# Attention over pairs of units: ScalarE instead of VectorE multiplies the second unit's probabilities by one over their sum

## The chip, the core and the metric

The kernel runs on one core of a Trainium2 chip, in one launch. The core has a matrix engine (TensorE, PE in the profile; its weight loads are PEld), three engines for elementwise work (VectorE or DVE, ScalarE or ACT, GpSimd or POOL) and a queue engine that issues transfers (SyncE, SP). Each runs its own list of instructions in order, and they wait for one another through semaphores. The metric is the device time of one execution in microseconds. Everything is computed in float32.

## The reference, cut to what matters

Two transformer layers over 256 latent tokens and 256 context tokens. Each layer has an attention, a recurrent half beside it, an output projection, and a mixture of experts, whose weights are most of the 497 MB that are read. What the change touches is the softmax of both attentions:

```python
def full_attention(q, k, v):                     # layer 0
    sc = jnp.einsum('bqhd,bkhd->bhqk', q, k).astype(F32) * q.shape[-1] ** -0.5
    p = jax.nn.softmax(sc, axis=-1).astype(v.dtype)
    return jnp.einsum('bhqk,bkhd->bqhd', p, v)

def window_attention(q, k, v, k_ctx, v_ctx, sink):   # layer 1
    ...
        p = jax.nn.softmax(jnp.concatenate([sk, s_ctx, s_band], axis=-1), axis=-1).astype(v.dtype)
        return (jnp.einsum('bkgqc,bckd->bqkgd', p[..., 1:1 + n_ctx], v_ctx)
                + jnp.einsum('bkgqs,bskd->bqkgd', p[..., 1 + n_ctx:], vi))
```

In layer 1 the window is applied by adding a mask to the scores, and a sink logit adds one more term to the sum of the exponentials.

## The kernel before, in words

The program is a chain of stages. Each is one block with a barrier at its end, so a stage starts when the last engine has finished the one before, and the loads of expert weights that a stage issues start with it. The two attention stages are calls of one function, `attention_stage` (L861).

A unit is one head and one tile of 128 queries. Layer 0 has 32 units: for the first 16 all 512 keys count ("wide"), for the other 16, whose queries are context tokens, only 256 ("narrow"). Layer 1 has 16 units of 512 keys. Two neighbouring units form a pair, the even unit first. A unit goes through these steps:

- `score` (L911): PE multiplies queries by keys into one of four PSUM banks (the trace shows four matmuls for a pair).
- `maximum` (L984): VectorE takes the row maximum (L995) and turns it into the bias of the exponential (L997; L1002 and L1003 where there is a sink). In layer 1 it first adds the mask (L991).
- `exponential` (L960): ScalarE takes the exponential and sums each row (L965); with a sink, one more small exponential (L968).
- normalisation (L1022 and L1023): VectorE takes the reciprocal of the sum (`den`) and multiplies the 128 rows of probabilities by it.
- `turn` (L918): PE transposes the probabilities, 128 by 128 at a time (L923). It waits for the multiplied probabilities.
- copy (L977): ScalarE copies the transposed probabilities out of PSUM.
- `values` (L926): PE multiplies them by the values of the pair (L933), and `copy_out` on VectorE takes the result out (L1009).

The order on each engine is written out by hand. PE, per round j: the scores of the next pair (2j+2, 2j+3), the turns of this pair (2j, 2j+1), the values of the pair before (j-1). In layer 0, in six of the rounds, PE also does a product for later modulation rows (L194), and VectorE adds its bias (L202, L206). ScalarE alternates: copy of unit u, exponential of unit u+2. VectorE, for each unit u: reciprocal and multiplication of u, then maximum of u+2; after the odd unit also the `copy_out` of the pair before.

Of the kernel before, what the change touches and what calls it, by code (L numbers as in the profile page):

```python
# [20 lines left out]
ALU = mybir.AluOpType  # L21
ACT = mybir.ActivationFunctionType
AX = mybir.AxisListType

P = 128
# [5 lines left out]
T = NT * P  # L31
# [21 lines left out]
class Chain:  # L53
# [6 lines left out]
    def step(self, ins):  # L60
        self.n += 1
        ins.then_inc(self.sem, 1)
        self.engine.wait_ge(self.sem, self.n)
# [797 lines left out]
def attention_stage(c, units, qt, kt, v_of, scale, dst_t, p, pt, width, sink=None, mask=None, sp_work=None, md=None):  # L861
# [4 lines left out]
    nc = c.nc  # L866
    n = len(units)
    pairs = n // 2
    scored, masked, nmax_r, exp_r, p_ready, turned, pt_ready, product, out_r = (
        c.sem(x) for x in ("scored", "masked", "negative_max", "exp_done", "probs_ready", "probs_turned", "probs_t_copied", "pv_product", "attn_copied"))  # L870
    den_r = c.sem("sink_exp")
    ada_after = {}
    if md:
        ada_after = {3 + a * (pairs - 6) // (md.n - 1): a for a in range(md.n)}
# [3 lines left out]
    nm, rs, es = ([c.stat[:, a + s:a + s + 1] for s in range(4)] for a in (0, 4, 8))  # L878

    def keys(u):  # L880
        return range(units[u][2], NT)

    with nc.Block() as block:
        @block.sync
        def _(sp):
            if md:
                for a in range(len(md.ring)):
                    if a == 1:
                        sp.wait_ge(tables_in, 16 * md.n_loads)
                    md.load_weights(sp, a, ada_in[a])  # L890
            if sp_work:
                sp_work(sp)
            if md:
                R = len(md.ring)
                for a in range(R, md.n):
                    sp.wait_ge(ada_product, a - R + 1)
                    md.load_weights(sp, a, ada_in[a % R])
                sp.wait_ge(ada_done, md.n)
                md.store(sp, stored)
                sp.wait_ge(stored, 16 * md.Q * len(md.segments))  # L900
# [8 lines left out]
        @block.tensor  # L909
        def _(pe):  # L910
            def score(u):  # L911
                h, t, k0 = units[u]
                if u >= 4:
                    pe.wait_ge(exp_r, u - 3)
                nc.tensor.matmul(c.ps[u % 4][:, k0 * P:T], qt[0:width, h, t * P:(t + 1) * P], kt(h)[0:width, k0 * P:T],
                                 start=True, stop=True).then_inc(scored, 1)

            def turn(u):  # L918
                pe.wait_ge(p_ready, u + 1)
                if u >= 2:  # L920
                    pe.wait_ge(pt_ready, u - 1)
                for k in keys(u):
                    last = nc.tensor.transpose(c.bank(4 + u % 2, 4, P)[:, k, :], p[:, u % 4, k * P:(k + 1) * P], c.ident[:])  # L923
                last.then_inc(turned, 1)

            def values(j):  # L926
                pe.wait_ge(pt_ready, 2 * j + 2)
                if j:
                    pe.wait_ge(out_r, j)
                for k in keys(2 * j):  # L930
                    for half in range(2):
                        u = 2 * j + half
                        last = nc.tensor.matmul(c.ps[6][half * 64:half * 64 + 64, 0:P], v_of(units[u][0], k), pt[:, u % 4, k, :],  # L933
                                                start=k == units[u][2], stop=k == NT - 1)
                last.then_inc(product, 1)

            score(0)
            score(1)
            for j in range(pairs):
                for u in (2 * j + 2, 2 * j + 3):  # L940
                    if u < n:
                        score(u)
                turn(2 * j)
                turn(2 * j + 1)
                if j:
                    values(j - 1)
                if j in ada_after:
                    a = ada_after[j]
                    if a == 0:
                        pe.wait_ge(columns, 1)  # L950
                    else:
                        pe.wait_ge(ada_done, a)
                    pe.wait_ge(ada_in[a % len(md.ring)], 16 * (a // len(md.ring) + 1))
                    md.product(a, 7).then_inc(ada_product, 1)
            values(pairs - 1)

        @block.scalar
        def _(act):
            def exponential(u):
                h, t, k0 = units[u]  # L960
                s = u % 4
                act.wait_ge(nmax_r, u + 1)
                if u >= 4:
                    act.wait_ge(turned, u - 3)
                nc.scalar.activation(p[:, s, k0 * P:T], c.ps[s][:, k0 * P:T], ACT.Exp, bias=nm[s], scale=scale,  # L965
                                     accum_out=rs[s]).then_inc(exp_r, 1)
                if sink is not None:
                    nc.scalar.activation(es[s], nm[s], ACT.Exp, bias=sink[:, h:h + 1]).then_inc(den_r, 1)  # L968

            exponential(0)  # L970
            exponential(1)
            for u in range(n):
                act.wait_ge(turned, u + 1)
                if u >= 4:
                    act.wait_ge(product, u // 2 - 1)
                k0 = units[u][2]
                nc.scalar.activation(pt[:, u % 4, k0:NT, :], c.bank(4 + u % 2, 4, P)[:, k0:NT, :], ACT.Copy).then_inc(pt_ready, 1)  # L977
                if u + 2 < n:
                    exponential(u + 2)

        @block.vector
        def _(dve):
            step = c.dve_chain.step
# [22 lines left out]
            def copy_out(j):  # L1006
                h, t, _ = units[2 * j]
                dve.wait_ge(product, j + 1)
                nc.vector.tensor_copy(dst_t[:, h // 2, t * P:(t + 1) * P], c.ps[6][:, 0:P]).then_inc(out_r, 1)  # L1009
# [5 lines left out]
            for u in range(n):  # L1015
                k0 = units[u][2]
                dve.wait_ge(exp_r, u + 1)
                den = rs[u % 4]
                if sink is not None:
                    dve.wait_ge(den_r, u + 1)  # L1020
                    step(nc.vector.tensor_tensor(den, den, es[u % 4], ALU.add))
                step(nc.vector.reciprocal(den, den))  # L1022
                nc.vector.tensor_scalar(p[:, u % 4, k0 * P:T], p[:, u % 4, k0 * P:T], den, None, ALU.mult).then_inc(p_ready, 1)  # L1023
                if u + 2 < n:
                    maximum(u + 2)
                j = u // 2
                if u % 2 and j:
                    copy_out(j - 1)
                    if j - 1 in ada_after:
                        if ada_after[j - 1] == 0:  # L1030
                            dve.wait_ge(tables_in, 16 * md.n_loads)
                        dve.wait_ge(ada_product, ada_after[j - 1] + 1)
                        md.finish(ada_after[j - 1], 7, ada_done)
# [1278 lines left out]
```

## Time and profile before

| what | value |
|---|---|
| median of three runs | 1686.78 us (1683.6 to 1687.5) |
| the profiled execution: its time, its span | 1687.27 us, 1685.5 us |
| mean granted TensorE clock over the span | 0.865 of full speed |
| PE, PEld busy | 1249.5 us (74%), 727.4 us (43%) |
| DVE, ACT, POOL busy | 541.3 us (32%), 405.3 us (24%), 39.3 us (2%) |
| layer 0's attention stage | from about 256 to 335 us |
| layer 1's attention stage | from about 1099 to 1161 us |

The two stages are 141 us of the span, 8%. In most of the rest the DMA share is 0.9 or more: the experts' weights are streamed. Inside the attention stages no weights of experts are loaded (the loads of layer 0's stage are modulation weights and the output projection), so shares over the whole span say little about them; they are read with views cut to their stretch. In a timeline row the idle time in brackets is what the engine waited just before the row, and what ended the wait.

### The profile page before, as it was taken

To read this page: it belongs to the slowest core of one execution; us is meant where nothing else is said; L and a number is where in the kernel's file an instruction comes from. 1 tells how busy PE (TensorE), PEld (TensorE's weight loads), DVE (VectorE), ACT (ScalarE), POOL (GpSimd) and SP (SyncE) were. 2 spreads that over 40 slices of the span, in tenths; PEclk is the share of its full clock that TensorE was granted. 3 is DMA by queue.
4 is the path that set the end of the run, shared out by engine and by line. 5 is a ranking of instruction groups with operands and counts; after the bars stand their busy time and mean duration, and the time that the engine had idled before them with its cause. 6 is when DMAs were issued, how large, how long until landed. Compare 5 with 4: busy or idle time off the path is not lost. (4 is left out here: it accounts for less than half of the span.)

```text
span 1685.5 us, 34940 instructions
## 1 busy us (share of the span) xinstructions
PE 1249.5 (74%) x14230; PEld 727.4 (43%) x14231; DVE 541.3 (32%) x1492; ACT 405.3 (24%) x932; POOL 39.3 (2%) x83
## 2 busy tenths in 40 slices
PE   3897888795799997686762999488497675556552
PEld 2454665543465554343431565244255342223221
DVE  0537555515322221121115444863521110111102
ACT  0343224303132321121104123342222221111110
POOL 0001001010000000000002000000000000000000
PEclk8899899997899998899875999758699897777776
DMA  6411988396699999999987210442689999999995
GB/s 254 156 76 45 329 331 305 106 408 254 254 415 428 429 430 428 429 429 429 429 354 256 68 50 0 168 182 88 257 365 428 429 429 429 429 429 429 429 429 217
DMA packets 84160, 515.12 MB, mean 306 GB/s; under 512 B 13917, under 2 KB 18242, under 8 KB 58746
## 3 DMA queue, kind: packets, MB, share of 16 engines
q1 hardware_dynamic: 75248, 489.63, 70.9%
q10 hardware_dynamic: 5146, 13.78, 2.1%
q0 software_dynamic: 3696, 10.73, 1.7%
q8 instruction: 50, 0.82, 0.2%
q14 instruction: 20, 0.16, 0.0%
HBM read 497.10 MB, written 17.01 MB: 305 GB/s over the span
## 5 line engine op out<-in xcount | busy, mean ns | idle before, releaser
L1481 PE MATMUL bank<-sb_ring,sb_scratch 128*32 128x256 f32 x3904 | 271.8, 440 | 150.7 <-DMA sb_ring<-in_moe_w_up 139.3
L1481 PEld LDWEIGHTS bank<-sb_ring,sb_scratch 128*32 128x32 f32 x3904 | 146.4, 126 | 273.6 <-issue 214.2
L1562 DVE TENSOR_TENSOR sb_scratch<-sb_scratch,bank 128x128 f32<-128x128 f32 x88 | 25.4, 288 | 701.2 <-ACT sb_scratch L1515 701.2
L1519 ACT ACTIVATE sb_scratch<-bank 32x256 f32<-32x256 f32 x352 | 131.8, 374 | 273.9 <-PE bank L1491 270.8
L1481 PE MATMUL bank<-sb_scratch 128*32 128x256 f32 x1728 | 117.5, 432 | 63.4 <-DMA sb_scratch<-in_moe_w_up 58.4
L1461 PE MATMUL bank<-sb_h,sb_scratch 128*32 128x256 f32 x2256 | 141.2, 385 | 6.1 <-DVE sb_scratch L1549 6.1
L1515 ACT ACTIVATE sb_scratch<-bank 128x128 f32<-128x128 f32 x88 | 24.4, 277 | 424.5 <-PE bank L1481 424.4
L1491 PE MATMUL bank<-sb_ring,sb_scratch 128*32 128x256 f32 x1856 | 111.5, 380 | 8.6 <-issue 8.2
L1481 PEld LDWEIGHTS bank<-sb_scratch 128*32 128x32 f32 x1728 | 61.5, 124 | 117.9 <-issue 92.7
L1461 PEld LDWEIGHTS bank<-sb_h,sb_scratch 128*32 128x32 f32 x2256 | 75.0, 111 | 54.6 <-DVE sb_scratch L1549 6.6
L1491 PEld LDWEIGHTS bank<-sb_ring,sb_scratch 128*32 128x32 f32 x1856 | 62.7, 110 | 51.2 <-issue 19.0
L1882 PE MATMUL bank<-sb_ht,sb_ring 128*128 128x512 f32 (+1 forms) x192 | 69.2, 521 | 0.0
L556 PE MATMUL bank<-sb_ht,sb_ring 128*128 128x512 f32 x128 | 55.3, 593 | 1.4 <-PEq L311 1.4
L1491 PE MATMUL bank<-sb_scratch 128*32 128x256 f32 x864 | 51.9, 380 | 4.6 <-issue 4.1
L1554 DVE STREAM_TRANSPOSE sb_scratch<-bank 128x256 f32<-128x256 f32 x90 | 38.9, 432 | 37.4 <-PE bank L1461 37.4
L1882 PEld LDWEIGHTS bank<-sb_ht,sb_ring 128*128 128x128 f32 x192 | 36.3, 190 | 31.3 <-issue 29.6
L194 PE MATMUL bank<-sb_ring 128*32 128x128 f32 x1280 | 40.2, 282 | 6.7 <-DMA sb_ring<-in_ada_w 6.7
L1066 PE MATMUL bank<-sb_ring,sb_scratch 128*128 128x512 f32 x96 | 43.2, 592 | 0.0
L194 PEld LDWEIGHTS bank<-sb_ring 128*32 128x32 f32 x1280 | 35.4, 113 | 13.5 <-DMA sb_ring<-in_ada_w 7.7
L1515 ACT ACT_TABLE_LOAD x21 | 26.9, 1283 | 56.3 <-issue 38.8
L1491 PEld LDWEIGHTS bank<-sb_scratch 128*32 128x32 f32 x864 | 29.2, 110 | 24.6 <-issue 9.7
L556 PEld LDWEIGHTS bank<-sb_ht,sb_ring 128*128 128x128 f32 x128 | 24.2, 190 | 31.6 <-issue 31.6
(366 smaller groups left out, 1450.4 us busy)
## 6 DMA issues: line engine op xcount, KB each, us to landing
sb_ring<-in_moe_w_gate SPq DMA_DIRECT2D x44, 2048.0 KB, 27.4
sb_ring<-in_moe_w_up SPq DMA_DIRECT2D x44, 2048.0 KB, 32.1
sb_ring<-in_moe_w_down SPq DMA_DIRECT2D x41, 2048.0 KB, 34.5
sb_ring<-in_ada_w SPq DMA_DIRECT2D x20, 2048.0 KB, 14.4
sb_scratch<-in_moe_w_up SPq DMA_DIRECT2D x20, 2048.0 KB, 35.7
sb_scratch<-in_moe_w_gate SPq DMA_DIRECT2D x20, 2048.0 KB, 29.9
sb_scratch<-in_moe_w_down SPq DMA_DIRECT2D x20, 2048.0 KB, 36.2
sorted_out<-sb_scratch ACTq DMA_DIRECT2D x88, 128.0 KB, 6.1
```

The lines of the kernel that those rows point to most:

```text
L194: last = self.c.nc.tensor.matmul(self.c.ps[bank][32 * q:32 * q + 32, 0:P], self.condk[:, k, :], w[:, k, q * P:(q + 1) * P], start=k == 0, ...
L556: last = nc.tensor.matmul(c.ps[u % NB][:, 0:rhs.shape[1]], lhs, rhs, start=k == 0, stop=k == KC - 1)
L1066: last = nc.tensor.matmul(c.ps[u % 4][:], src, wo[:, k, q * BANK:(q + 1) * BANK], start=k == 0, stop=k == KC - 1)
L1461: last = nc.tensor.matmul(c.ps[0][MB * q:MB * q + MB, 0:DQ], m.pick[:, t, :], c.h[:, t, q * DQ:(q + 1) * DQ], start=t == 0, stop=t == nt - 1)
L1481: last = nc.tensor.matmul(c.bank(1, 2, FQ)[MB * q:MB * q + MB, :, :], m.xt[:, k, :], m.gu[j][:, :, k, q * FQ:(q + 1) * FQ], start=k == 0, ...
L1491: last = nc.tensor.matmul(c.ps[3][MB * q:MB * q + MB, 0:DQ], m.hmt[:, k, :], down[k][:, q * DQ:(q + 1) * DQ], start=k == 0, stop=k == DE / ...
L1515: nc.scalar.activation(m.sg, c.ps[1][:, 0:FQ], ACT.Silu).then_inc(silu_r, 1)
L1519: last = nc.scalar.activation(m.yb[j][:, q * DQ:(q + 1) * DQ], c.ps[3][MB * q:MB * q + MB, 0:DQ], ACT.Copy)
L1554: v.transpose(m.xt, c.bank(0, MB, KC).rearrange("p j k -> p k j")).then_inc(xt_ready, 1)
L1562: v.tensor_tensor(m.hm, m.sg, c.ps[1][:, FQ:2 * FQ], ALU.mult).then_inc(hm_ready, 1)
L1882: last = nc.tensor.matmul(c.ps[bank_of(u)][:, 0:rhs.shape[1]], lhs, rhs, start=k == 0, stop=k == KC - 1)
```

## The change

For every odd unit VectorE only takes the reciprocal (after.py L1036) and signals it through a new semaphore, `inverse_sum`. ScalarE waits for it, multiplies the probabilities in place by the reciprocal (`divide`, after.py L977 to L980: a Copy whose scale is the column of reciprocals) and signals `odd_probs_ready`, for which PE's turn of an odd unit now waits. The even units stay as they were. ScalarE's list is written in another order, by pairs. The line numbers after L966 move by 2 to 16.

```diff
             def turn(u):
-                pe.wait_ge(p_ready, u + 1)
+                pe.wait_ge(odd_ready if u % 2 else p_ready, u // 2 + 1)
...
-            exponential(0)
-            exponential(1)
-            for u in range(n):
+            def copy_turned(u):
                 act.wait_ge(turned, u + 1)
                 if u >= 4:
                     act.wait_ge(product, u // 2 - 1)
...
-                if u + 2 < n:
-                    exponential(u + 2)
+
+            def divide(u):
+                k0 = units[u][2]
+                act.wait_ge(inverse_r, u // 2 + 1)
+                nc.scalar.activation(p[:, u % 4, k0 * P:T], p[:, u % 4, k0 * P:T], ACT.Copy, scale=rs[u % 4]).then_inc(odd_ready, 1)
+
+            exponential(0)
+            exponential(1)
+            divide(1)
+            for j in range(pairs):
+                copy_turned(2 * j)
+                if j + 1 < pairs:
+                    exponential(2 * j + 2)
+                    exponential(2 * j + 3)
+                copy_turned(2 * j + 1)
+                if j + 1 < pairs:
+                    divide(2 * j + 3)
...
-                step(nc.vector.reciprocal(den, den))
-                nc.vector.tensor_scalar(p[:, u % 4, k0 * P:T], p[:, u % 4, k0 * P:T], den, None, ALU.mult).then_inc(p_ready, 1)
+                if u % 2:
+                    nc.vector.reciprocal(den, den).then_inc(inverse_r, 1)
+                else:
+                    step(nc.vector.reciprocal(den, den))
+                    nc.vector.tensor_scalar(p[:, u % 4, k0 * P:T], p[:, u % 4, k0 * P:T], den, None, ALU.mult).then_inc(p_ready, 1)
```

ScalarE's list in layer 0's attention, wide units, over two rounds, before (L965 is the exponential, L977 the copy of turned probabilities; `sb_scratch` holds the probabilities, `sb_stat` their sums):

```order
L977 ACTIVATE sb_h<-bank 128x512
L965 ACTIVATE sb_scratch,sb_stat<-bank,sb_stat 128x512
L977 ACTIVATE sb_h<-bank 128x512
L965 ACTIVATE sb_scratch,sb_stat<-bank,sb_stat 128x512
L977 ACTIVATE sb_h<-bank 128x512
L965 ACTIVATE sb_scratch,sb_stat<-bank,sb_stat 128x512
```

and after, in the same place (L975 is the copy, L980 the new multiplication):

```order
L980 ACTIVATE sb_scratch<-sb_scratch,sb_stat 128x512
L975 ACTIVATE sb_h<-bank 128x512
L965 ACTIVATE sb_scratch,sb_stat<-bank,sb_stat 128x512 x2
L975 ACTIVATE sb_h<-bank 128x512
L980 ACTIVATE sb_scratch<-sb_scratch,sb_stat 128x512
```

One instruction per pair is added, it stands ahead of the even unit's copy, and the two exponentials now stand together between the two copies.

VectorE's list in the same stretch, before (L1022 the reciprocal, L1023 the multiplication, L995 and L997 the maximum, L1009 the copy out):

```order
L1009 COPY sb_h<-bank 128x128
L1022 RECIPROCAL sb_stat<-sb_stat 128x1
L1023 TENSOR_SCALAR sb_scratch<-sb_scratch,sb_stat 128x512
L995 TENSOR_REDUCE sb_stat<-bank 128x1
L997 TENSOR_SCALAR sb_stat<-sb_stat 128x1
L1022 RECIPROCAL sb_stat<-sb_stat 128x1
L1023 TENSOR_SCALAR sb_scratch<-sb_scratch,sb_stat 128x512
L995 TENSOR_REDUCE sb_stat<-bank 128x1
L997 TENSOR_SCALAR sb_stat<-sb_stat 128x1
```

and after (L1036 is the odd unit's reciprocal, L1038 and L1039 the even unit's reciprocal and multiplication, L1008 and L1010 the maximum, L1022 the copy out):

```order
L1022 COPY sb_h<-bank 128x128
L1038 RECIPROCAL sb_stat<-sb_stat 128x1
L1039 TENSOR_SCALAR sb_scratch<-sb_scratch,sb_stat 128x512
L1008 TENSOR_REDUCE sb_stat<-bank 128x1
L1010 TENSOR_SCALAR sb_stat<-sb_stat 128x1
L1036 RECIPROCAL sb_stat<-sb_stat 128x1
L1008 TENSOR_REDUCE sb_stat<-bank 128x1
L1010 TENSOR_SCALAR sb_stat<-sb_stat 128x1
```

The odd unit's multiplication is gone; its reciprocal still stands behind the maximum of the next even unit.

## Rows read from the trace of the kernel before

**Rows 1.** Windows: both attention stages, then three stretches of layer 1's.
```profile
core 0: us, PE busy (x) PEld busy (x) DVE busy (x) ACT busy (x) POOL busy (x), PEclk, DMA share, GB/s
256.00:335.00 79.00, 66.20 (x736) 43.16 (x736) 45.36 (x155) 34.56 (x97) 5.40 (x10) 0.96 0.59 215
1099.00:1161.00 62.00, 54.07 (x227) 30.27 (x228) 35.75 (x120) 24.68 (x66) 0.00 (x0) 0.64 0.24 102
1117.65:1125.33 7.68, 7.68 (x31) 4.17 (x29) 4.44 (x15) 2.79 (x8) 0.00 (x0) 0.50 0.01 2
1140.50:1143.50 3.00, 2.23 (x8) 0.79 (x6) 2.43 (x9) 0.73 (x2) 0.00 (x0) 1.00 0.00 0
1144.00:1147.00 3.00, 3.00 (x21) 2.34 (x21) 1.15 (x4) 1.67 (x6) 0.00 (x0) 0.50 0.00 0
```

**Rows 2.** Waits in layer 0's attention: total us, times, longest us.
```profile
PEld bank L923 <- DVE sb_scratch L1023: 18.7, 24, 1.3
```

**Rows 3.** Timeline, PE, a wide round: start us, us, instruction, idle before.
```profile
269.48 1.98 PE L915 MATMUL bank<-sb_scratch,sb_ht 96*128 96x512 f32 x4
271.30 0.60 PE L923 MATMUL bank<-sb_ident,sb_scratch 128*128 128x128 f32 x4
272.41 0.66 PE L923 MATMUL bank<-sb_ident,sb_scratch 128*128 128x128 f32 x4 [0.51 <-DVE sb_scratch L1023]
...
274.02 1.99 PE L915 MATMUL bank<-sb_scratch,sb_ht 96*128 96x512 f32 x4
```

**Rows 4.** Timeline, DVE, the same round.
```profile
270.65 0.69 DVE L995 TENSOR_REDUCE sb_stat<-bank 128x1 f32<-128x512 f32 x1 [0.16 <-PE bank L915]
...
271.67 0.16 DVE L1022 RECIPROCAL sb_stat<-sb_stat 128x1 f32<-128x1 f32 x1
271.87 0.49 DVE L1023 TENSOR_SCALAR sb_scratch<-sb_scratch,sb_stat 128x512 f32<-128x512 f32 x1
...
274.14 0.29 DVE L1009 COPY sb_h<-bank 128x128 f32<-128x128 f32 x1 [1.00 <-PE bank L933]
274.35 0.15 DVE L1022 RECIPROCAL sb_stat<-sb_stat 128x1 f32<-128x1 f32 x1
```

**Rows 5.** Timeline, ACT, the same round.
```profile
271.94 0.60 ACT L977 ACTIVATE sb_h<-bank 128x512 f32<-128x512 f32 x1 [2.11 <-PE bank L923]
...
273.01 0.20 ACT L965 ACTIVATION_READ_ACCUMULATOR sb_scratch<-bank,sb_stat 128x1 f32 x1
```

**Rows 6.** ACT groups by form: xcount | busy us, mean ns | idle.
```profile
L2009 ACT ACTIVATE sb_h<-sb_h 128x512 f32<-128x512 f32 x8 | 5.0, 630 | 24.0 <-DVEq L2057 24.0
...
L1645 ACT ACTIVATE sb_scratch<-sb_scratch,sb_wsel 128x1024 f32<-128x1024 f32 x4 | 4.6, 1144 | 14.4 <-DMA sb_scratch<-sorted_out,sb_slot 14.4
L1649 ACT ACTIVATE sb_h<-sb_x 128x1024 f32<-128x1024 f32 x4 | 4.2, 1052 | 1.8 <-DVE sb_x L1689 1.8
...
L1999 ACT ACTIVATE sb_scratch<-sb_scratch 128x256 f32<-128x256 f32 x7 | 3.0, 429 | 0.0
```

**Rows 7.** ACT groups by form: the copies of wide turned probabilities.
```profile
L977 ACT ACTIVATE sb_h<-bank 128x512 f32<-128x512 f32 x16 | 9.6, 597 | 19.2 <-PE bank L923 19.1
```

**Rows 8.** Timeline, DVE then ACT: a hand-over from one to the other.
```profile
208.31 0.17 DVE L428 TENSOR_SCALAR sb_stat<-sb_stat 128x8 f32<-128x8 f32 x1
...
208.51 0.21 ACT L808 ACTIVATE sb_stat<-sb_stat 128x8 f32<-128x8 f32 x1 [0.52 <-DVE sb_stat L428]
```

**Rows 9.** Timeline, DVE: the multiplication of a narrow odd unit.
```profile
312.75 0.35 DVE L1023 TENSOR_SCALAR sb_scratch<-sb_scratch,sb_stat 128x256 f32<-128x256 f32 x1
```

**Rows 10.** Timeline, PE, layer 1: a round at half clock, then a mixed one.
```profile
1117.65 3.78 PE L915 MATMUL bank<-sb_scratch 64*128 64x512 f32 x4
1121.37 2.13 PE L923 MATMUL bank<-sb_ident,sb_ring 128*128 128x128 f32 x8
...
1143.94 1.11 PE L923 MATMUL bank<-sb_ident,sb_ring 128*128 128x128 f32 x4 [1.20 <-DVE sb_ring L1023]
...
1150.80 1.12 PE L923 MATMUL bank<-sb_ident,sb_ring 128*128 128x128 f32 x4 [1.21 <-DVE sb_ring L1023]
```

**Rows 11.** Timeline, DVE, the half-clock round: the odd unit's multiplication.
```profile
1121.83 0.49 DVE L1023 TENSOR_SCALAR sb_ring<-sb_ring,sb_stat 128x512 f32<-128x512 f32 x1
```

More of the change, by code:

```diff
@@ L870, in attention_stage @@
         c.sem(x) for x in ("scored", "masked", "negative_max", "exp_done", "probs_ready", "probs_turned", "probs_t_copied", "pv_product", "attn_copied"))
-    den_r = c.sem("sink_exp")
+    den_r, inverse_r, odd_ready = c.sem("sink_exp"), c.sem("inverse_sum"), c.sem("odd_probs_ready")
     ada_after = {}
```

## The prediction

> **What bounds the kernel now.** The page says little: VectorE is busy 32% and ScalarE 24% of the span, but most of the span streams experts' weights. I cut the views to the two attention stages. By windows, layer 0's stage runs at a granted clock of 0.96 with PE busy 66 of 79 us [rows 1]. So PE is close to being the bound, and what counts is where it waits. The waits name it: weight loads of the turns (L923) wait 24 times, 18.7 us in all, for VectorE's multiplication L1023 [rows 2].
>
> The timeline of one wide round shows which multiplication. PE does the scores of the next pair, then the even unit's turn at once; then it is idle 0.51 us and starts the odd unit's turn at 272.41 [rows 3]. VectorE ended the odd unit's multiplication at 271.87 + 0.49 = 272.36 [rows 4]. That is late because VectorE, in order, first takes the maximum of the next even unit, whose scores are ready only when this round has begun: the reduce starts at 270.65 behind a wait for PE, the odd reciprocal at 271.67 [rows 4]. After the values PE goes straight into the next round, 274.02 - 269.48 = 4.54 us after this one. The loop is closed: scores, maximum, odd reciprocal, odd multiplication, odd turn, values, scores. Whatever lengthens the time from the odd reciprocal to the odd turn lengthens every round by as much. The narrow rounds and layer 1 have the same order; there PE waits 1.20 us for the odd multiplication in the later rounds [rows 10]. In layer 1's rounds at half clock PE is busy throughout [rows 1], and the two turns follow without a gap [rows 10].
>
> **The change, part by part.** Removed: 24 multiplications on VectorE (8 wide and 8 narrow in layer 0, 8 in layer 1). Added: 24 multiplications on ScalarE and a hand-over from VectorE to it. Both stand on the loop.
>
> *Old piece.* Reciprocal start to multiplication start 0.20, multiplication 0.49: 0.69 us for a wide unit [rows 4]. Narrow: the multiplication takes 0.35 [rows 9], so 0.20 + 0.35 = 0.55.
>
> *New piece.* The reciprocal itself 0.16 [rows 4]. The hand-over: VectorE ended at 208.31 + 0.17 = 208.48, ScalarE started at 208.51, so 0.03 [rows 8]. The multiplication: a wide activation from SBUF to SBUF takes 0.630; one whose scale is a column of SBUF took 1.144 against 1.052 without it at 1024 elements, so the column costs 0.09 [rows 6]. Together 0.72. Narrow: 0.429 + 0.09 = 0.52 [rows 6]. So 0.16 + 0.03 + 0.72 = 0.91 wide and 0.71 narrow: **+0.22** per wide, **+0.16** per narrow pair.
>
> *The bounds of that price.* No row has exactly this form. From below, the copy out of PSUM without a column, 0.597 [rows 7], would give 0.16 + 0.03 + 0.60 - 0.69 = +0.10 wide, and 0.429 without the column +0.07 narrow. From above, the nearest longer row of the form is the 1.144 for twice the elements [rows 6], +0.42 more for each. I take 0.72 and 0.52, because the size and the column are each shown by a pair of rows.
>
> The Trainium skill, VectorE: DVE Perf Modes, section The TRN2 errata, gives (224 + N)/1.2 ns for ScalarE from SBUF and (58 + N/2)/0.96 ns for a VectorE copy or multiplication in its double mode. For 512 that is 0.61 and 0.33, for 256 0.40 and 0.19. The trace agrees on ScalarE (0.63) and not on VectorE (0.49 and 0.35); by the page an estimate of the loss would be +0.27 and +0.20 a pair, 5.8 us where the rows give 4.6. The measured rows decide.
>
> *The sum.* Layer 0: 8 x 0.22 + 8 x 0.16 = 3.0. Layer 1: in six of its eight rounds PE waits for the odd multiplication, 6 x 0.22 = 1.3. In two half-clock rounds, as that from 1117.65, the second turn starts half way through 2.13 us, at 1122.43 [rows 10], and the multiplication had ended at 1122.32 [rows 11]: 0.11 hides half of it, 2 x 0.11 = 0.2. Sum 3.0 + 1.3 + 0.2, unrounded **+4.6 us**.
>
> *ScalarE's other work.* ScalarE was idle 2.11 us before the even copy at 271.94 [rows 5], so the multiplication finds it free. It stands ahead of that copy: reciprocal done at 271.83, ScalarE held from 271.86 for 0.72, to 272.58, so the even copy and the next even exponential come at most 0.6 us late. That exponential's sum was done at 273.21 [rows 5]; the reciprocal that needs it started at 274.35 [rows 4]. The slack of 1.14 covers 0.6. The odd copy comes behind both exponentials now; those who need it, the pair's values and the bank's next turn, stand in the next round behind its scores. Cost nothing; if that cover were gone, up to 0.6 a round.
>
> *What VectorE gains.* 0.49 us a wide unit, 0.35 a narrow one. It comes behind the odd reciprocal, so it makes the maximum of the next odd unit early, and then VectorE waits for the values anyway, 1.00 us before the copy out [rows 4]. The gain falls into that wait: nothing.
>
> *Transfers.* No transfer moves. Each stage starts its loads at its own start, behind a barrier, so the delay passes to the end whole.
>
> *The clock.* Layer 1's stage has a granted clock of 0.64 in the mean. Its early rounds run at half clock; the later ones are mixed: scores at the full 2.4 GHz (granted 1.00), and after the wait for the odd multiplication the odd turn and values at 1.2 GHz (granted 0.50) [rows 1]. A mixed round takes 1150.80 - 1143.94 = 6.86 us [rows 10], one at half clock throughout 7.68 [rows 1]. The clock fell each time around the 1.20 us wait and came back after a stretch without one. With 1.42 us of waiting and another period, I expect it to come back less often: two of the four late rounds at half clock, 2 x (7.68 - 6.86) = +1.6. Bounds: none, or all four plus the last turns and values at half rate, about +6; and below nothing, -1.6, if it comes back two rounds earlier.
>
> Forecast: 4.6 + 1.6 = **+6.2 us**. The profiled execution took 1687.27 (span 1685.5 and 1.8 around it), 0.5 above the median of 1686.78; on the median that is **1693**.
>
> **The rivals.**
> *B, only the price, no clock.* +4.6, or +2.0 with the lower price (14 x 0.10 + 8 x 0.07, and nothing in the two half-clock rounds). Then 1689 to 1691.4, within 0.3% (5.1 us, about what a measurement of this kernel tells from no change). For it: the clock's share is the weakest term. Against: rows 6 pin the price.
> *C, the clock drops further.* Layer 0's stage is at 0.96 in the mean [rows 1], though PE waits in every round. If the added 0.2 us makes it swing as in layer 1, each fall doubles the piece behind the wait, 274.02 - 272.41 = 1.6 us [rows 3]. Three falls (4.8) and all four late rounds of layer 1 at half clock (4 x 0.82 = 3.3) give 4.6 + 4.8 + 3.3, some +13, 1699.5. The Trainium skill, TensorE: Matmul & The Clock Gate, section A second HAM failure mode, says that brief idles between groups of matmuls can make the clock swing; layer 1 here shows it, layer 0 does not.
> *D, faster: VectorE is the bound and its relief counts.* If the next maxima were what PE waits for, 16 x 0.49 + 8 x 0.35 = 10.6 us would be freed against 4.6 lost: -6.0, 1681. It decides where the VectorE time behind the odd reciprocal is followed by no wait. Against it: the 1.00 us of wait there [rows 4]; only rounds in which VectorE adds a modulation bias have less.
> That the change does not do what it says I rule out: VectorE's list has the multiplication gone and ScalarE's has one activation for it.
>
> **How the numbers follow.** A 0.50, C 0.12, B 0.34, D 0.04. A and C are slower by over 0.3%, B is within, D faster. The range from 1687.5 to 1699 holds A and B but for B's lowest corner, and leaves out D and most of C. All of it is one sign but for D.
>
> **What would show it.** The odd turn starts 0.2 us later behind the scores than before; a ScalarE row of 0.72 and 0.52 us; the wait before it 0.7 in a wide round, 1.4 in layer 1; wide rounds of 4.76 us; VectorE's wait before the copy out about 0.6 us longer; the even exponential 0.5 us later without a reader waiting; layer 1's granted clock under 0.64. It is wrong if the odd turn starts no later, if the wide round stays at 4.54, or if the two stages together are not 5 to 7 us longer.

## The result and the profile after

| | before | changed kernel |
|---|---|---|
| median | 1684.51 us (8 runs, 1682.91 to 1687.5) | 1692.13 us (8 runs, 1690.46 to 1696.49) |
| profiled execution: time, span | 1687.27, 1685.5 us | 1692.91, 1690.7 us |
| mean granted TensorE clock | 0.865 | 0.859 |

The ratio is 1.0044, with a 95% interval from 1.0033 to 1.0056: slower by more than 0.3%. The forecast was 1693 us. It stood on a median of 1686.78 us for the kernel before; as a difference, 6.2 us were forecast and the medians differ by 7.6, the two profiled executions by 5.6.

The first thing to read is where the 5.2 us between the two spans lie. I cut each execution at four instructions that both have: the first scores of each attention stage and the first matmul of the output stage behind it.

| part | before | changed kernel | difference |
|---|---|---|---|
| layer 0's attention | 256.38 to 335.31: 78.93 | 256.47 to 338.56: 82.09 | +3.16 |
| between the stages | 764.37 | 764.22 | -0.15 |
| layer 1's attention | 1099.68 to 1159.94: 60.26 | 1102.78 to 1162.93: 60.15 | -0.11 |
| from there to the end | 525.56 | 527.77 | +2.2 |

The wide round in layer 0, on PE (start us, us, instruction, idle before):

```profile
270.13 1.98 PE L915 MATMUL bank<-sb_scratch,sb_ht 96*128 96x512 f32 x4
271.95 0.60 PE L923 MATMUL bank<-sb_ident,sb_scratch 128*128 128x128 f32 x4
273.30 0.66 PE L923 MATMUL bank<-sb_ident,sb_scratch 128*128 128x128 f32 x4 [0.74 <-ACT sb_scratch L980]
...
274.91 1.98 PE L915 MATMUL bank<-sb_scratch,sb_ht 96*128 96x512 f32 x4
...
315.65 0.44 PE L923 MATMUL bank<-sb_ident,sb_scratch 128*128 128x128 f32 x2 [0.90 <-ACT sb_scratch L980]
```

These answer to [rows 3]. The odd turn starts 3.17 us behind the scores, not 2.93, and waits 0.74 us where it waited 0.51. The wait is now for ScalarE's L980. The round is 274.91 - 270.13 = 4.78 us against 4.54. The last row is a narrow odd turn: it waited 0.75 before. Eight times 0.24 and eight times 0.15 are 3.1, the 3.16 of the stage.

The waits of the turns' weight loads in that stage (total us, times, longest us) answer to [rows 2]:

```profile
PEld bank L923 <- ACT sb_scratch L980: 17.0, 16, 1.3
...
PEld bank L923 <- DVE sb_scratch L1039: 5.1, 8, 1.3
```

Together 22.1 us against 18.7, which is 3.4 us more; the stage grew by 3.16. VectorE in the same round, which answers to [rows 4]:

```profile
272.32 0.16 DVE L1036 RECIPROCAL sb_stat<-sb_stat 128x1 f32<-128x1 f32 x1
272.43 0.69 DVE L1008 TENSOR_REDUCE sb_stat<-bank 128x1 f32<-128x512 f32 x1
...
275.02 0.29 DVE L1022 COPY sb_h<-bank 128x128 f32<-128x128 f32 x1 [1.72 <-PE bank L933]
275.23 0.15 DVE L1038 RECIPROCAL sb_stat<-sb_stat 128x1 f32<-128x1 f32 x1
```

and ScalarE, which answers to [rows 5]:

```profile
272.52 0.72 ACT L980 ACTIVATE sb_scratch<-sb_scratch,sb_stat 128x512 f32<-128x512 f32 x1 [1.74 <-DVE sb_stat L1036]
...
274.19 0.20 ACT L965 ACTIVATION_READ_ACCUMULATOR sb_scratch<-bank,sb_stat 128x1 f32 x1
```

The hand-over took 272.52 - 272.48 = 0.04 us. VectorE's freed time went into the wait before the copy out, 1.00 to 1.72. The even exponential's sum is done at 274.39, and its reader starts at 275.23: 0.84 us of slack are left. ScalarE's new instruction by its form (layer 0's stage):

```profile
L980 ACT ACTIVATE sb_scratch<-sb_scratch,sb_stat 128x512 f32<-128x512 f32 x8 | 5.8, 722 | 16.6 <-DVE sb_stat L1036 16.6
L980 ACT ACTIVATE sb_scratch<-sb_scratch,sb_stat 128x256 f32<-128x256 f32 x8 | 4.1, 508 | 19.0 <-DVE sb_stat L1036 19.0
```

It takes 0.722 and 0.508 us; 0.72 and 0.52 had been put together from other rows.

Layer 1, PE, from the second round of half clock on. These answer to [rows 10]:

```profile
1120.84 3.78 PE L915 MATMUL bank<-sb_scratch 64*128 64x512 f32 x4
...
1128.87 2.42 PE L915 MATMUL bank<-sb_scratch 64*128 64x512 f32 x4
...
1136.27 2.14 PE L915 MATMUL bank<-sb_scratch 64*128 64x512 f32 x4
...
1140.43 1.11 PE L923 MATMUL bank<-sb_ident,sb_ring 128*128 128x128 f32 x4 [1.44 <-ACT sb_ring L980]
...
1143.38 2.00 PE L915 MATMUL bank<-sb_scratch 64*128 64x512 f32 x4
...
1147.40 0.66 PE L923 MATMUL bank<-sb_ident,sb_ring 128*128 128x128 f32 x4 [1.44 <-ACT sb_ring L980]
...
1149.01 1.98 PE L915 MATMUL bank<-sb_scratch 64*128 64x512 f32 x4
```

The wait grew from 1.20 to 1.44, as priced: a mixed round is 1143.38 - 1136.27 = 7.11 us, before 6.90 (1146.89 - 1139.99 in that trace). But the round from 1143.38 is of a kind that the kernel before does not have: turn (0.66 for four, not 1.11) and values at the full clock too, in spite of the wait, 5.63 us. Set round by round beside each other, the stage differs by +0.24 up to the scores at 1112.94, then -0.15, +0.35, -0.27, +0.12, -1.27 and +0.87, together -0.11. The clock also rose one round sooner: the scores of 1128.87 take 2.42 us, where the kernel before has a third round at half clock (7.67 us) and the clock rises in the scores of 1133.00. The longer wait was paid in the late rounds, and given back by one round without a fall of the clock. The last part, from 1149.01 on, ran partly at half clock and took 0.87 us more. The windows show it in the mean:

```profile
1103.00:1163.00 60.00, 50.64 (x225) 28.53 (x225) 31.62 (x112) 28.72 (x73) 0.00 (x0) 0.66 0.23 96
...
1143.38:1149.01 5.63, 4.19 (x30) 2.38 (x29) 3.93 (x14) 2.38 (x6) 0.00 (x0) 0.99 0.00 0
```

The clock is 0.66 here against 0.64 [rows 1]. A second profiled execution of the changed kernel, below, has the same rounds to within 0.02 us.

The +2.2 us at the end begin 55 us behind layer 1's attention, where the experts' first matmuls run. The same 20 us of before and then of the changed kernel (columns as in [rows 1]):

```profile
1214.94:1234.94 20.00, 15.25 (x234) 8.19 (x238) 6.25 (x30) 3.34 (x7) 0.00 (x0) 0.82 0.60 239
```

```profile
1217.93:1237.93 20.00, 15.14 (x206) 7.87 (x210) 5.12 (x25) 3.34 (x7) 0.00 (x0) 0.73 0.53 210
```

PE is as busy, at 0.73 instead of 0.82 of its clock, and has done 28 matmuls less; the loads bring 210 instead of 239 GB/s.

### The profile page after: what moved, and what is told of

The parts are those of the page before. It is cut to its first block and busy times, and to the rows that moved or that the text cites. A ratio compares the mean times of both kernels' runs of the same rounds, so it can differ in the third digit from the quotient of the medians.

```text
span 1690.7 us, 34940 instructions
## 1 busy us (share of the span) xinstructions
PE 1248.7 (74%) x14230; PEld 728.3 (43%) x14231; DVE 530.6 (31%) x1468; ACT 417.4 (25%) x956; POOL 39.4 (2%) x83
```

## The experiments

Eleven more kernels ran, and the changed one once more, each beside runs of the kernel before on the same chip; the ratios are to those, whose medians were 1685.67 us (order alone, one layer at a time, even units), 1686.08 us (early reciprocals with one or no unit on ScalarE, constant scale, halves) and 1686.08 us (filled, both units on ScalarE, the same again).

| kernel | median us | ratio, 95% interval | layer 0 | layer 1 | rest |
|---|---|---|---|---|---|
| before | 1684.51 | | 78.9 | 60.3 | 1546.3 |
| changed kernel | 1692.13 | 1.0044, 1.0033 to 1.0056 | 82.1 | 60.2 | 1548.5 |
| the same again | 1693.38 | 1.0033, 1.0018 to 1.0048 | 82.2 | 60.1 | 1548.9 |
| ScalarE's order alone | 1688.06 | 1.0010, 0.9999 to 1.0020 | 79.2 | 60.3 | 1548.9 |
| only in layer 0 | 1688.87 | 1.0016, 1.0000 to 1.0032 | 82.2 | 56.5 | 1545.3 |
| only in layer 1 | 1688.89 | 1.0012, 0.9999 to 1.0024 | 79.0 | 59.1 | 1545.6 |
| even units on ScalarE | 1679.77 | 0.9970, 0.9954 to 0.9987 | 76.9 | 53.0 | 1541.7 |
| early reciprocals, VectorE | 1665.46 | 0.9877, 0.9857 to 0.9897 | 68.1 | 49.1 | 1547.4 |
| early reciprocals, ScalarE | 1661.75 | 0.9865, 0.9846 to 0.9884 | 68.6 | 44.8 | 1545.0 |
| constant scale | 1692.81 | 1.0049, 1.0032 to 1.0065 | 81.9 | 55.5 | 1551.9 |
| in halves | 1703.12 | 1.0113, 1.0093 to 1.0133 | 89.5 | 62.0 | 1548.7 |
| before, wait filled | 1679.35 | 0.9963, 0.9945 to 0.9981 | 79.4 | 49.8 | 1550.6 |
| changed, wait filled | 1684.90 | 0.9993, 0.9981 to 1.0004 | 82.5 | 54.3 | 1546.5 |
| both units on ScalarE, early | 1662.28 | 0.9864, 0.9844 to 0.9884 | 69.7 | 45.1 | 1543.9 |

Layer 0, layer 1 and the rest are stage times in the one profiled execution of each, cut as above; the rest is its span without the two stages. The rest moves by several us between kernels that differ in nothing there, so single small differences of it carry no verdict. A stage time is that of one execution, and the spread of a kernel's executions can be wider than what the stages show: those of the kernel with the even units on ScalarE lie between 1673.8 and 1688.7 us, and the profiled one is the fastest of them.

### The order alone

VectorE multiplies every unit again; only ScalarE's list keeps its new order.

```diff
-                pe.wait_ge(odd_ready if u % 2 else p_ready, u // 2 + 1)
+                pe.wait_ge(p_ready, u + 1)
...
-            divide(1)
...
-                if j + 1 < pairs:
-                    divide(2 * j + 3)
```

> ScalarE keeps the new order (even copy, both exponentials, odd copy) but VectorE multiplies the odd units again, as in the kernel before. Theory 1 (the loss is the longer piece between the odd reciprocal and the odd turn): this piece is back to 0.69 us, the wide round back to 4.54 us, the time that of the kernel before within 0.1%. Rival 2 (the loss comes from ScalarE's new order, which makes the odd copy 0.7 us later): most of the 7.5 us stays, 1.003 or more. Rival 3 (the clock in layer 1 alone): the time as before in layer 0, and anything up to 3 us in layer 1.

```profile
269.61 1.98 PE L915 MATMUL bank<-sb_scratch,sb_ht 96*128 96x512 f32 x4
...
272.55 0.66 PE L923 MATMUL bank<-sb_ident,sb_scratch 128*128 128x128 f32 x4 [0.51 <-DVE sb_scratch L1033]
```

The odd turn is back at 2.94 us behind the scores, the wait at 0.51, and both stages within 0.3 us of before. The order costs the loop nothing. The +0.1% of the time is not told from no change; neither attention stage shows it.

### One layer at a time

```diff
-                if u % 2:
+                if sink is None and u % 2:
                     nc.vector.reciprocal(den, den).then_inc(inverse_r, 1)
```

with the same condition at PE's wait and at the two calls of `divide`: only layer 0. The other kernel has `sink is not None`.

> ScalarE multiplies the odd units in layer 0's attention only; layer 1 has ScalarE's new order but VectorE's multiplication. Theory 1: +3.2 us in layer 0 (8 x 0.22 + 8 x 0.16 and the first round), nothing in layer 1, so 1.0019. Rival 2: +3.2 and layer 1's share stays, 1.003 to 1.0045. Rival 3: layer 0 costs nothing, 1.000.

> ScalarE multiplies the odd units in layer 1's attention only; layer 0 has ScalarE's new order but VectorE's multiplication. Theory 1: +1.5 us for the price and about +1.6 for rounds that stay at half clock, together about +3, 1.0018; without the clock term 1.0009. Rival 3 (the clock in layer 1 is most of the loss): +4 us or more, 1.0025. Rival 2: 1.003 or more.

Layer 0's stage is longer by 3.2 us where ScalarE multiplies there and by 0.0 where not. Layer 1's does not follow: with VectorE's multiplication it took 60.3 us in the order alone and 56.5 in the kernel that differs from that one only in layer 0. The same instructions ran at a granted clock of 0.63 and of 0.70. So one profile of layer 1 cannot price a change of 1.5 us; the clock moves it by more. The medians put about as much on either layer (0.16% and 0.12%), neither clear of no change, and their sum of 0.28% falls short of 0.44% and 0.33%, within the intervals.

### The even unit on ScalarE

```diff
-                pe.wait_ge(odd_ready if u % 2 else p_ready, u // 2 + 1)
+                pe.wait_ge(p_ready if u % 2 else odd_ready, u // 2 + 1)
...
-                if u % 2:
+                if u % 2 == 0:
```

and `divide(2 * j + 2)` behind the odd unit's copy and exponential.

> The even units instead of the odd ones: ScalarE multiplies each even unit behind the odd exponential, VectorE makes only its reciprocal there and multiplies the odd ones. Theory 1: in a wide round the even turn has a slack of 0.8 us (multiplication done at 270.49, turn at 271.30), the longer even piece (+0.22) fits in it, and the loop through the odd unit is untouched: the wide round stays at 4.54 us. In the narrow rounds in which VectorE adds a modulation bias the even turn waits for VectorE, so there up to +0.16, or a gain where the next maximum starts 0.27 earlier. Time within 0.15% of the kernel before. If any multiplication on ScalarE costs its 0.2 us wherever it stands (rival 4), 1.003 or more, as in the changed kernel.

The time missed what was expected (within 0.15%): it fell by 0.3%. The wide odd turn waits 0.51 for VectorE as before. Layer 0 became 2.0 us shorter all the same, 1.4 of it in the four rounds with narrow scores in which VectorE adds a modulation bias, and 0.5 in the first two rounds of the stage. The kernel before and then this one:

```profile
314.12 1.13 PE L915 MATMUL bank<-sb_scratch,sb_ht 96*128 96x256 f32 x4
315.57 0.44 PE L923 MATMUL bank<-sb_ident,sb_scratch 128*128 128x128 f32 x2 [0.32 <-DVE sb_scratch L1023]
...
317.74 1.96 PE L194 MATMUL bank<-sb_ring 128*32 128x128 f32 x64
```

```profile
310.18 1.13 PE L915 MATMUL bank<-sb_scratch,sb_ht 96*128 96x256 f32 x4
311.78 0.44 PE L923 MATMUL bank<-sb_ident,sb_scratch 128*128 128x128 f32 x2 [0.47 <-ACT sb_scratch L980]
...
313.40 1.95 PE L194 MATMUL bank<-sb_ring 128*32 128x128 f32 x64
```

3.62 us became 3.22. There the copy out, two bias instructions, the even reciprocal and the even multiplication stand ahead of the next maximum, and the multiplication is gone. The forecast's rival D, relief of VectorE, is real for the even unit and in these rounds. In layer 1 the third, fourth and fifth round run at the full clock with the 1.20 us wait still in them; in the sixth the clock falls behind the same wait (its values take 1.98 us and not 1.09):

```profile
1110.35 1.98 PE L915 MATMUL bank<-sb_scratch 64*128 64x512 f32 x4
...
1114.12 0.66 PE L923 MATMUL bank<-sb_ident,sb_ring 128*128 128x128 f32 x4 [1.20 <-DVE sb_ring L1038]
...
1115.73 1.98 PE L915 MATMUL bank<-sb_scratch 64*128 64x512 f32 x4
...
1126.50 1.98 PE L915 MATMUL bank<-sb_scratch 64*128 64x512 f32 x4
...
1130.97 1.98 PE L933 MATMUL bank<-sb_ring,sb_scratch 128*64 128x128 f32 x16
```

The third to the fifth round take 5.38 us each, where the kernel before takes 6.9 or 7.7: that is where most of the stage's 7 us went, and it is the clock. The first two rounds, at half clock in both kernels, give 1.0 us more. All this is the fastest of ten executions.

### Both reciprocals ahead of the maxima

VectorE's list is written by pairs: normalise the even and the odd unit, then both maxima, then the copy out. Once with VectorE's multiplications alone, once as the changed kernel has them.

```diff
-            for u in range(n):
+            def normalise(u):
...
+            for j in range(pairs):
+                normalise(2 * j)
+                normalise(2 * j + 1)
+                if j + 1 < pairs:
+                    maximum(2 * j + 2)
+                    maximum(2 * j + 3)
```

> VectorE does all the multiplications, as before the change, but in a round it takes reciprocal and multiplication of both units first and the two maxima of the next pair after them, so the odd multiplication no longer stands behind a maximum that waits for PE. ScalarE has the new order. Theory 1 (the loop is closed by the place of the odd reciprocal behind the next even maximum): PE's wait before the odd turn goes: wide rounds 4.54 to about 4.03, narrow ones by up to 0.7, layer 1's mixed rounds by up to 1.2 and its clock stays higher. At least 10 us faster, 0.994 or less. Rival 4 (VectorE's work as such is the bound): the maxima come later by what the multiplications came earlier, no gain, 1.000.

> The changed kernel (ScalarE multiplies the odd units) with both reciprocals ahead of the maxima of the next pair. Theory 1: the odd multiplication is ready before the scores end, so its longer piece (+0.22) is hidden, and the relief of VectorE (0.49 us a pair) counts at last where VectorE is the longer: as fast as e5 or faster, 0.994 or less. Rival 4 (a multiplication on ScalarE costs its 0.2 us wherever it stands): 4 to 5 us slower than e5. A middle case: where ScalarE holds the even copy back behind the multiplication, up to 0.3 us a round is lost against e5.

The second, PE:

```profile
269.09 1.98 PE L915 MATMUL bank<-sb_scratch,sb_ht 96*128 96x512 f32 x4
270.91 1.04 PE L923 MATMUL bank<-sb_ident,sb_scratch 128*128 128x128 f32 x8
271.88 1.09 PE L933 MATMUL bank<-sb_h,sb_ring 128*64 128x128 f32 x16
272.91 1.98 PE L915 MATMUL bank<-sb_scratch,sb_ht 96*128 96x512 f32 x4
```

In the wide rounds the wait is gone, eight transposes in a row: 3.82 us a round. In layer 1 waits of 0.23 to 0.39 us for ScalarE are left. This cuts the loop that the forecast named, and it is worth 23 us, 1.35%. In the profiles layer 0 is 10.3 us shorter at about the same clock (0.95 for 0.96), and layer 1 is 15.4 us shorter with the clock at 0.82 for 0.63; how much of the latter is the clock was not separated. Now the price that the change pays does not count: 1.0044 turned into 0.9865, beside 0.9877 for VectorE alone. The two intervals overlap.

### The price itself, smaller and larger

A constant for the column of reciprocals; the odd units are left unnormalised:

```diff
-... ACT.Copy, scale=rs[u % 4]).then_inc(odd_ready, 1)
+... ACT.Copy, scale=1.0).then_inc(odd_ready, 1)
```

> The changed kernel, but ScalarE's multiplication takes the constant 1.0 in place of the column of reciprocals: the odd units are left unnormalised, the waits stay. Theory 1: the instruction takes 0.63 instead of 0.72 us (0.43 instead of 0.51 narrow), the wait before the odd turn is 0.09 us shorter in each of 24 rounds, 2 us faster than the changed kernel: 1.003 against the kernel before. If the price of the change is in the hand-over or in the order (rival 2), no difference from the changed kernel, 1.0044.

```profile
268.06 1.98 PE L915 MATMUL bank<-sb_scratch,sb_ht 96*128 96x512 f32 x4
...
271.13 0.66 PE L923 MATMUL bank<-sb_ident,sb_scratch 128*128 128x128 f32 x4 [0.65 <-ACT sb_scratch L980]
...
272.74 1.98 PE L915 MATMUL bank<-sb_scratch,sb_ht 96*128 96x512 f32 x4
```

The column costs 0.09 us (629 against 722 ns), and wait and round (4.68) are 0.09 and 0.10 shorter. The stage as a whole is only 0.2 us shorter, since at its end the clock falls (two groups of eight values at 1.12 us, not 0.66) where it does not in the changed kernel. The total missed what was expected, 1.0049 and not 1.003, and says little about the price: the data behind the softmax are other ones here, and the stretch between the stages took 771.6 us instead of 764.2. The cause of that is open.

The multiplication in two halves:

```diff
+                half = (k0 * P + T) // 2
+                nc.scalar.activation(p[:, u % 4, k0 * P:half], ..., scale=rs[u % 4])
+                nc.scalar.activation(p[:, u % 4, half:T], ..., scale=rs[u % 4]).then_inc(odd_ready, 1)
```

> The changed kernel with ScalarE's multiplication cut in two halves of 256 (128 narrow) elements, one after the other. An activation with a column took 0.72 for 512 and 0.51 for 256, so two of 256 take about 1.0 less 0.1 of overlap: +0.2 us a wide pair, and 0.40 + 0.30 = about 0.7 less 0.1: +0.1 to 0.2 a narrow pair. Theory 1: every such 0.1 us shows in the wait before the odd turn and in the round, the loss is about doubled: another 4 us, 1.0065 against the kernel before. Rival 3 (the clock) or rival 2 (order): no more than the changed kernel, 1.0044.

The wide odd turn waits 0.93 us, 0.19 more than in the changed kernel, the narrow ones 1.09 to 1.12, again 0.19 more. Sixteen times that is 3.0, but the stage is 7.4 us longer. The rest is the clock: it falls in two of the narrow rounds and in the last turns of the stage, as it does nowhere in the changed kernel's. So the loss grew by more than was expected, to 1.0113 and not 1.0065. The halves first, then the changed kernel:

```profile
318.00:332.00 14.00, 10.56 (x112) 7.32 (x110) 6.42 (x27) 5.97 (x23) 0.00 (x0) 0.88 0.01 2
```

```profile
318.00:332.00 14.00, 11.19 (x178) 8.23 (x178) 6.36 (x27) 5.90 (x21) 0.00 (x0) 1.00 0.01 2
```

```profile
321.68 0.44 PE L923 MATMUL bank<-sb_ident,sb_scratch 128*128 128x128 f32 x2 [1.11 <-ACT sb_scratch L982]
322.04 0.98 PE L933 MATMUL bank<-sb_h,sb_ring 128*64 128x128 f32 x8
322.96 3.24 PE L194 MATMUL bank<-sb_ring 128*32 128x128 f32 x64
```

The last fence, PE in the halves, shows a fall: the 64 small matmuls behind the values take 3.24 us and not 1.95. This is the forecast's rival C, with the wait 0.2 us longer than the change made it. In the other six narrow rounds the clock stayed up behind waits of the same length.

### The wait filled

Four products of the identity with itself, into a bank that nobody reads, between the even and the odd turn of layer 1; in the kernel before and in the changed one.

```diff
                 turn(2 * j)
+                if sink is not None:
+                    for _ in range(4):
+                        nc.tensor.matmul(c.ps[7][:, 0:P], c.ident[:], c.ident[:], start=True, stop=True)
                 turn(2 * j + 1)
```

> The kernel before, with four extra matmuls (identity by identity, into an unused bank) between the even and the odd turn in layer 1's attention: work that nobody reads, put into PE's wait for the odd multiplication. About 0.6 us a round at full clock, inside the 1.20 us of wait. Theory 3 (the clock falls around this wait and costs layer 1 several us): the clock stays at 1.00 once it has risen, rounds of 5.4 us in place of 6.86 and 7.68, 4 to 8 us faster, 0.9965. If the clock does not hang on the wait: four times 8 matmuls more, 0 to +4 us.

> The changed kernel with the same four extra matmuls. With the clock held at full in both, the difference from the filled kernel before is the pure price of the longer odd piece: 3.2 us in layer 0 and 7 or 8 x 0.22 = 1.7 in layer 1, +4.9 us. If part of the changed kernel's 7.5 us is the clock in layer 1, the two filled kernels differ by less than the two unfilled ones; if theory 1 alone holds and the clock has no part, by as much.

The kernel before, filled, and then the changed one, filled:

```profile
1123.87 1.98 PE L915 MATMUL bank<-sb_scratch 64*128 64x512 f32 x4
...
1127.64 0.66 PE L923 MATMUL bank<-sb_ident,sb_ring 128*128 128x128 f32 x4 [0.32 <-DVE sb_ring L1026]
...
1129.25 1.98 PE L915 MATMUL bank<-sb_scratch 64*128 64x512 f32 x4
```

```profile
1127.58 1.98 PE L915 MATMUL bank<-sb_scratch 64*128 64x512 f32 x4
...
1131.59 0.66 PE L923 MATMUL bank<-sb_ident,sb_ring 128*128 128x128 f32 x4 [0.55 <-ACT sb_ring L983]
...
1133.20 1.98 PE L915 MATMUL bank<-sb_scratch 64*128 64x512 f32 x4
```

Work that nobody needs makes both faster, by 0.4% each (from 1 to 0.9963, and from 1.0033 to 0.9993). The products fit into the wait, 0.32 and 0.55 us of it are left, and the clock does not fall behind it: 5.38 us a round, and 5.62. Where the clock is up in both, the price can be read in layer 1 as well: 5.62 - 5.38 = 0.24 a round, in the fourth to the sixth round. Those rounds are the cleanest measurement of the forecast's first term. The clock is not alike in the whole stage, which takes 54.3 us in one and 49.8 in the other: 3.1 of the 4.5 us between them is the second round, 8.90 us at half clock in the filled changed kernel and 5.77 in the other. The last two rounds together take the same, 12.11 and 12.10 us: in the very last one the turn that waits is the even unit's, 1.42 us in the filled kernel before and 1.18 in the filled changed one, and that gives back what the round ahead of it pays. The medians differ by 5.5 us, where the unfilled kernels on the same chip differ by 7.3; the intervals of the ratios are too wide to say that filling made the difference smaller.

### Both units on ScalarE, and the changed kernel again

Early reciprocals, and ScalarE multiplies the even units too, so VectorE has no multiplication left.

```diff
-                if u % 2:
-                    nc.vector.reciprocal(den, den).then_inc(inverse_r, 1)
-                else:
-                    ...
+                nc.vector.reciprocal(den, den).then_inc(inverse_r, 1)
```

> As e6 (both reciprocals ahead of the next maxima), with ScalarE multiplying the even units too. VectorE is relieved of another 0.49 us a pair, which should count in layer 1, where PE waits 0.23 to 0.31 us for ScalarE and VectorE in e6, and ScalarE gets 0.63 more a round, 3.7 of 3.8 us in a wide round. Theory 1: whoever comes last sets the round; with ScalarE this full, it is now the bound in wide rounds: within 2 us of e6, rather slower. If VectorE is the bound in e6: another 3 to 5 us faster.

0.9864 against 0.9865: behind early reciprocals, moving the second multiplication as well gives nothing. It was expected within 2 us of the kernel with early reciprocals that moves only the odd one.

> The changed kernel once more, so that it shares runs of the kernel before with the two filled ones: 1.0044 as measured, and another look at which rounds of layer 1 run at half clock. Layer 0's stage again 3.2 us longer than before; layer 1's stage anywhere from 57 to 63 us by the clock.

Twelve runs, with a median of 1693.38; four of them lie between 1686.78 and 1690.66, the others from 1693.0 up. The profile is that of the first one: stage times within 0.1 us, and the same kinds of rounds in layer 1. The ratio is 1.0033, with an interval from 1.0018 that reaches below 0.3%. What makes the four faster was not seen, since the profiled execution was not one of them. It stays open.

## Why the prediction was right, and where it was not

The total came out close, and the loop and its price were right. But the forecast had named a sign of being wrong, the two stages together not 5 to 7 us longer, and by it it was wrong: its second term, the clock, had the wrong sign, and what made up for it was not in the forecast. That the sum was right was in part luck.

**The loop, and what stands on it: right, and shown.** The odd turn starts 0.24 us later behind the scores (0.2 forecast). With the multiplication back on VectorE it starts where it did; with the reciprocal taken out from behind the maximum the wait is gone, with 21 to 23 us, the clock's part in layer 1 included; with the piece made 0.1 shorter or 0.2 longer the wait follows.

**The price per unit: right.** 0.22 and 0.16 were forecast; PE's waits grew by 0.23 and 0.15. The 0.72 put together from an activation's time and the price of a column is 0.722; the column's 0.09 is 0.093 by the constant scale. For layer 0 3.0 us had been forecast and 3.16 came. For layer 1 1.5 had been forecast, and an estimate from the rows gives about 1.2: 0.44 in the first three rounds, at half clock in both kernels (26.09 us against 25.65), 3 x 0.24 in the next three, and nothing in the last two together, by the filled pair. What the forecast had wrong there is the last round: it counted it as paying, and the even turn that waits in it gains. The 24 waits of 18.7 us that the forecast read as the odd multiplication's include eight of even turns, 5.1 us in the changed kernel.

An estimate from the figures of the Trainium skill, VectorE: DVE Perf Modes, section The TRN2 errata, put the price at 5.8 us in all, and at 8 x 0.27 + 8 x 0.20 = 3.8 us for layer 0. The trace does not agree: layer 0 lost 3.16, near the 3.0 of the rows.

**What hides the rest: right.** The even exponential's sum comes 0.53 us later behind the scores with 0.84 left, VectorE's wait before the copy out took the freed time (0.72 longer), and the stretch between the two stages kept its length (-0.15 us). It holds for the odd unit only: behind the even unit's multiplication stands a maximum that PE does need, in the narrow rounds with a modulation bias.

**The clock: the step that failed.** It said: "With 1.42 us of waiting and another period, I expect it to come back less often: two of the four late rounds at half clock, 2 x (7.68 - 6.86) = +1.6." The wait had its 1.44 us, but the clock rose one round sooner, and one late round did not fall at all: 0.66 in the mean instead of under 0.64. The stage changed by -0.11 us with a price of 1.2 (rows) to 1.5 (forecast) in it, so the clock's term was -1.3 to -1.6 and not +1.6. That is at or near the lower bound that the forecast had given for it. So the two stages together are 3.05 us longer and not 5 to 7.

**What no step had in it.** The total of the profiles came with the 2.2 us behind layer 1's attention, a stretch that no step of the forecast looked at, and the medians differ by another 2 us that stand in no profile. In that stretch the clock was lower in the first experts' matmuls of the changed kernel (0.73 for 0.82), and the second profile repeats it, with 528.3 us to the end. What sets it was not isolated. With the order alone, only in layer 0 and only in layer 1 the time from layer 1's attention to the end is 525.4, 524.9 and 526.0 us, so it is not simply the delay. Nor does it need the change: the kernel before with the wait filled took 527.7 us there, at 0.81 in the same 20 us. The cause of the 2.2 us stays open.

How far the sign of the clock's term was luck shows in the table: for one and the same code in layer 1, with VectorE's multiplications and ScalarE's new order, the stage took 60.3 or 56.5 us. Whether that comes from how the program arrives at the stage was not isolated; the changed kernel's two profiles are alike to 0.1 us. The size of the clock's effect is shown too: filling the wait brings 6 to 7 us in the kernel before.

**The rivals.** B (price only) holds what the loop did, about 4.4 us of its 4.6. By the ratio of the first comparison the result lies above it (5.6 to 9.4 us), by the second both fit (3.0 to 8.1). C did not happen in layer 0 with this change, and did in two rounds and at the end with 0.2 us more. D was false for the odd unit; for the even one it held in a few rounds of layer 0.

**What beats both kernels.** The changed kernel with both reciprocals ahead of the maxima: 1661.75 us against 1686.08 on the same chip, by the ratio 1.35% faster than before. Which engine multiplies then hardly matters. Early reciprocals together with the filled wait were not tried.

## What to carry to other kernels

Before moving an instruction to a freer engine, look at what stands in front of it: here the odd multiplication was late because its reciprocal queued behind a maximum that waits for PE, and putting both reciprocals ahead of the maxima was worth about three times what the move of the multiplication cost. A busy share of 24% or 32% says nothing about it; the wait of the engine that closes the loop, and the instruction ahead of the releaser, do. Where the granted clock swings in a stage, price its waits at either level, keep the clock's term as a range of both signs, and do not read a change of 1 or 2 us there from one profile.

## What the runs showed of the hardware that was not expected

The length of a wait alone did not decide whether TensorE's clock fell from 2.4 GHz (granted 1.00) to 1.2 (granted 0.50). In layer 1 it fell behind 1.20 us of waiting in each of the three late rounds of the kernel before; with the even unit on ScalarE it stayed up behind three such waits in a row and fell at the fourth. Behind 1.44 us in the changed kernel it fell twice, stayed up once and fell again among the values behind the next; behind 1.34 us, with the constant scale, it fell once and then stayed up three times. In layer 0's narrow rounds it stayed up behind all waits of 0.90 to 0.93 us, and fell at two of the eight of 1.09 to 1.12.

Four products of no use in the wait, 1.06 us in the trace's row, kept the clock up in all but the first one or two rounds. They brought 0.4%, 6 to 7 us by the ratios.

An activation whose scale is a column took 93 ns more than one with a constant, at 512 elements as at 1024 (92). In two halves it took 508 + 492 ns instead of 722, but the turn came only 0.19 us later, since the second half starts 0.41 us after the first:

```profile
271.30 0.51 ACT L981 ACTIVATE sb_scratch<-sb_scratch,sb_stat 128x256 f32<-128x256 f32 x1 [1.75 <-DVE sb_stat L1038]
271.71 0.49 ACT L982 ACTIVATE sb_scratch<-sb_scratch,sb_stat 128x256 f32<-128x256 f32 x1
```
